# Reordering one RWKV-7 round: k's products behind the second powers, the rates' low-rank product ahead of them, the identity sums behind the state's update

## What is computed

```python
def rwkv7_scan(r, w, k, v, a, b, state):      # a = -kk, b = kk * rate, 16 heads of 64
    def step(S, inp):
        r_t, w_t, k_t, v_t, a_t, b_t = inp
        sa = jnp.einsum('bhvk,bhk->bhv', S, a_t)
        S = S * w_t[:, :, None, :] + sa[..., None] * b_t[:, :, None, :] + v_t[..., None] * k_t[:, :, None, :]
        return S, jnp.einsum('bhvk,bhk->bhv', S, r_t)
...
w_log = -jax.nn.softplus(-(rw_w0[d] + jnp.tanh(w_low[..., d, :]) @ rw_w2[d])) - 0.5
a = jax.nn.sigmoid(rw_a0[d] + a_low[..., d, :] @ rw_a2[d])      # the rate
k_d = k * (1 + (a - 1) * rw_ka)
```

## Time and profile before

| what | value |
|---|---|
| median of three executions | 2301.28 us |
| the profiled execution's own time | 2312.86 us |
| its span on the core | 2310.8 us |
| TensorE (PE) busy | 1985.9 us, 86% of the span |
| VectorE (DVE) busy | 923.6 us, 40% |
| ScalarE (ACT) busy | 687.9 us, 30% |
| GpSimd (POOL) busy | 323.1 us, 14% |
| mean granted TensorE clock | 0.917 of full |
| RWKV rounds | from 1443.4 to 1836.4 us after the span's start |

### The profile page before, as it was taken

One profiled execution on the slowest core, in us unless ns is written; L12 is line 12 of the kernel. 1 busy time (PEld: TensorE's weight loads), 2 busy tenths in 40 slices (PEclk: granted clock), 3 DMA queues, 4 the chain that ended last, 5 costly groups with the idle time before them and its releaser, 6 DMA issues. The chain is left out here.

```text
span 2310.8 us, 54088 instructions
## 1 busy us (share of the span) xinstructions
PE 1985.9 (86%) x23877; PEld 1376.1 (60%) x23877; DVE 923.6 (40%) x1660; ACT 687.9 (30%) x1509; POOL 323.1 (14%) x210
## 2 busy tenths in 40 slices
PE   6999998997979888998578798799998897977775
PEld 3777765445854444555344587788988755634443
DVE  3193235586041111111235478466767443111102
ACT  3234534574230000100133343644543312000001
POOL 1433310001401000000100245221221000000000
PEclk8999999799979998999888999799999977988888
DMA  8554533203354798678820131000000125899975
GB/s 297 188 207 146 183 145 134 86 0 110 109 217 187 255 348 323 242 267 316 303 86 27 37 104 34 3 4 4 4 4 4 58 65 217 303 385 358 359 292 182
DMA packets 133312, 380.86 MB, mean 165 GB/s; under 512 B 14394, under 2 KB 43670, under 8 KB 115926
## 3 DMA queue, kind: packets, MB, share of 16 engines
q1 hardware_dynamic: 114528, 343.82, 40.4%
q10 hardware_dynamic: 15094, 20.99, 3.0%
q0 software_dynamic: 3456, 12.58, 1.5%
HBM read 634.54 MB, written 25.95 MB: 286 GB/s over the span
## 5 line engine op out<-in xcount | busy, mean ns | idle before, releaser
L371 PE MATMUL banks<-parts 128*128 128x512 f32 (+1 forms) x1096 | 244.0, 374 | 14.6 <-POOL parts L1523 7.6
L1814 PE MATMUL banks<-arena 128*32 128x256 f32 x1696 | 218.8, 403 | 38.1 <-DMA arena<-in_exp_w_up_dram 38.1
L371 PEld LDWEIGHTS banks<-parts 128*128 128x128 f32 x1096 | 194.1, 191 | 55.0 <-POOL parts L2388 9.5
L1815 PE MATMUL banks<-arena 128*32 128x256 f32 x1696 | 218.7, 403 | 0.0
L1880 ACT ACTIVATE arena<-banks 64x256 f32<-64x256 f32 x78 | 29.7, 380 | 556.9 <-PE banks L1815 371.1
L1814 PEld LDWEIGHTS banks<-arena 128*32 128x32 f32 x1696 | 102.1, 116 | 119.1 <-DMA arena<-in_exp_w_up_dram 42.1
L371 PE MATMUL banks<-arena,ring 128*128 128x256 f32 (+2 forms) x560 | 163.9, 460 | 9.4 <-PEq L318 8.5
L379 DVE TENSOR_TENSOR arena<-banks,arena 64x256 f32<-64x256 f32 (+3 forms) x136 | 71.0, 522 | 230.5 <-ACT arena L1880 145.1
L2005 DVE COPY arena<-banks 128x256 f32<-128x256 f32 x78 | 33.1, 425 | 323.3 <-DMA y_sorted<-arena 244.0
L1836 PE MATMUL banks<-arena 128*32 128x256 f32 x1696 | 117.5, 424 | 43.2 <-DVE arena L1995 24.6
L371 PEld LDWEIGHTS banks<-arena,ring 128*128 128x128 f32 (+1 forms) x560 | 108.7, 199 | 60.9 <-issue 47.6
(11 more groups left out here) (371 smaller groups left out, 3712.6 us busy)
## 6 DMA issues: line engine op xcount, KB each, us to landing
arena<-in_exp_w_gate_dram SPq DMA_DIRECT2D x106, 1024.0 KB
arena<-in_exp_w_up_dram SPq DMA_DIRECT2D x106, 1024.0 KB
arena<-in_exp_w_down_dram SPq DMA_DIRECT2D x53, 2048.0 KB
ring<-in_exp_w_gate_dram SPq DMA_DIRECT2D x50, 1024.0 KB
ring<-in_exp_w_up_dram SPq DMA_DIRECT2D x50, 1024.0 KB
ring<-in_exp_w_down_dram SPq DMA_DIRECT2D x25, 2048.0 KB
ring<-in_w_mod_dram SPq DMA_DIRECT2D x24, 2048.0 KB, 9.0
ring<-in_ab_w_in_dram SPq DMA_DIRECT2D x10, 2048.0 KB, 13.7
```

Of the source, the lines that this page charges most:

```text
L371: m = nc.tensor.matmul(o, a, b, start=first and n == 0, stop=last and n == len(pairs) - 1)
L1814: nc.tensor.matmul(o[r:r + BLOCK, 0:256], x, up[:, k, c], start=k == 0, stop=k == KD - 1)
L1815: m = nc.tensor.matmul(o[64 + r:64 + r + BLOCK, 0:256], x, gate[:, k, c], start=k == 0, stop=k == KD - 1)
```

## The change

In `pe_round` the AK product (in segment 1 the pair AK RK) is taken and issued behind D2t, and za is taken and issued ahead of D2, in AK's old place. In `dve_round` the masks of AK (and RK) stand behind the scans of the decays; the two sums T1 are taken out of `dve_head` and put behind the state's update (and, in segment 1, behind the addition of Y). In `pool_round` a wait for the AK product is added ahead of "A ka". `act_round` is as it was.

```diff
@@ pe_round
                     both("W1 Xt", ("a", "S b"), parts=("W1", "Xt"))
-                    if seg == 1:
-                        take_pair("AK RK", "AK", "RK")
-                        both("AK RK", ("k", "a r"), parts=("AK", "RK"))
-                    else:
-                        take("AK")
-                        both("AK", ("k", "a"))
+                if front:
+                    take("za")
+                    low_rank("za", b_a2, b_al)
+                if main:
                     take("D2")
...
                         each("D2t", [("D", "Dt")], g)
-                if front:
-                    take("za")
-                    low_rank("za", b_a2, b_al)
                 if main:
+                    if seg == 1:
+                        take_pair("AK RK", "AK", "RK")
+                        both("AK RK", ("k", "a r"), parts=("AK", "RK"))
+                    else:
+                        take("AK")
+                        both("AK", ("k", "a"))
                     take_pair("D4 T2", "D4", "T2")
@@ dve_head
                         masked("RB", "RB", g, 1, "RB read")
+
+            def dve_sum():
                 for g in range(2):
                     go(vadd(now[g]["T"], now[g]["D"], stackid[:].unsqueeze(1).to_broadcast([P, 8, L])), g, "T1")
@@ dve_round
+                if front:
+                    for d in range(2):
+                        scan_decay(d)
+                if main:
                     for g in range(2):
                         masked("AK", "AK", g, 0, "AK read")
                         if seg == 1:
                             masked("RK", "RK", g, 1, "RK read")
-                if front:
-                    for d in range(2):
-                        scan_decay(d)
-                if main:
...
                 if seg == 1:
                     onto_output("Y")
+                if front:
+                    following["dve sum"]()
@@ pool_round
                 g = nc.gpsimd.tensor_tensor
+                for x in range(2):
+                    pool.wait_ge(*at_(("AK product", x)))
```

More of the change, by code:

```diff
@@ L2956, in rwkv_round @@
             return {"front": front, "pe": pe_round, "act": act_round, "dve": dve_round, "pool": pool_round, "pe decay": pe_decay,
-                    "act decay": act_decay, "pe head": pe_head, "dve head": dve_head}
+                    "act decay": act_decay, "pe head": pe_head, "dve head": dve_head, "dve sum": dve_sum}
         def rwkv_chunks():
```

## The result

The changed kernel is **slower by 1.6%**: a median of 2341.7 us in four executions (2340.4 to 2344.7) against 2303.9 for the kernel before in the same session, ratio 1.0163, 95% interval 1.0139 to 1.0186. Measured once more beside an experiment it came to 2337.7 against 2307.0, ratio 1.0137 (1.0114 to 1.0161). The forecast was 2338, range 2317 to 2357.

The account below looks back on a forecast made before the run. TensorE's in-order list was taken as the bound. Waits +9.5 and +16.5, T1 -5.4 and clock +15.3 sum to +35.9 us on the 2301.28 median: 2337, rounded to 2338, range 2317 to 2357.

Parts of the forecast that it names:

- The banks: Hand count: D4 T2 waits for za's readers in rounds 1-4; in 5-7 AK RK does, and D4 T2 for its masks.
- Rival 4: Banks turn differently from the count, D4 T2 owes no late reader, stalls ahead of D2 go: -9 us, 2292; chance 0.06.
- Segment 0: Rounds 1 to 4: D4 T2 waits for za's tanh after 3.0 us idle, +2.4 us a round, +9.5 for four.
- Segment 1: Rounds 5 to 7: AK RK idles 3.9 us, D4 T2 2.9; +5.5 us a round, +16.5 for three; round 8 zero.
- The clock: TensorE's clock falls at each of ten new idle times, 1.7 us each, less round 4's: +15.3 us, bounds 0 and +34.
- Rival 3: Bank waits, and the clock stays low twice as long after them: +53 us, 2354; chance 0.13.
- The sum: Whole kernel: waits and T1 +20.6 us plus clock +15.3 make +35.9, giving 2337, rounded to 2338.
- T1: Two sums moved behind the state's update let W1 Xt start sooner in rounds 2 to 7: -5.4 us.
- At nothing: AK's masks behind the scans, GpSimd's new wait ahead of "A ka", and round 8 were each put at no cost.
- Rival 5: Late waits exist but most time is given back later, as in stalls ahead of N or S: +5 us, 2306; chance 0.06.
- Rivals 2 and 3: Rival 2: bank waits, but the clock stays up in nearly all: +20.6 us, 2322; chance 0.17. Rival 3 has its own line.

Follow-up runs that it names:

- experiment 4: The changed kernel with only PSUM bank numbers altered, same instructions in the same order: 2305.1 us, ratio 1.0004 to the kernel before.
- experiment 3: Kernel before with the new order of AK and za in one segment only, T1 as before: rounds 1 to 4 alone 2318.0 us, rounds 5 to 8 alone 2326.3.

## Why the prediction was right

**The banks.** The count by hand held in every round: all ten waits (four, three and three) came where it put them, released by the instructions it named. Rival 4 (another turn of the banks) is out, and experiment 4 shows that the turn alone makes the loss.

**Segment 0.** D4 T2 was put at 11.6 us behind W1 Xt and 3.0 of idle time; it came at 11.85 to 12.14 and 3.12. From W1 Xt to D4 T2 the four rounds took 48.1 us against 39.0, +9.1, where +9.5 was forecast (four times 2.42 is 9.7). That the sums agree so well is in part luck: in rounds 1 and 2 the delay is 2.7 us each, and in rounds 3 and 4 only 1.8 and 2.0, because there the kernel before had lost time itself, by 1.22 us of idle time without a releaser and by the clock's fall of the earlier trace rows.

**Segment 1.** The idle times were put at 3.9 and 2.9, and came as 4.06 and 3.13; D4 T2 was put at 16.4 without the clock and came there at 17.0 in the kernel with filled waits.

**The clock.** The price of one fall was right: 1.7 us was forecast, 1.7 was measured behind D4 T2 (experiment 3), and six waits in segment 1 cost 10.5 us where six times 1.7 (10.2) was forecast. The number of falls was not right. In segment 0 four were forecast; in the changed kernel's profile the clock fell behind none of the four waits for the tanh, in its second profile behind two, in the profile of the order in segment 0 and in both profiles of the order alone behind three, in the one with filled waits behind one. The step that put the clock's fall at every wait failed there: behind the same 3.1 us it fell in twelve of 24 cases, and what decides it stays open. Rival 3 was right on one thing: in round 6 the clock stayed low through both waits, for 13.6 us. But that round's price was 4.0 us, against 3.1 and 3.3 in its neighbours, and not twice as much. The Trainium skill ("TensorE: Matmul & The Clock Gate", "A second HAM failure mode: psum-queue depth-cycling") says that a kernel cycling through PSUM banks can let TensorE idle briefly so often that its clock swings between the two levels. The trace agrees in direction: with the banks alone changed the low stretches went away. It doesn't agree at each wait.

**The sum.** +35.9 was forecast, and the rounds grew by 34.3 us in the changed kernel's profile; the medians give 37.8 and 30.7. By segment the forecast was less good than in sum: rounds 1 to 4 grew by 10.0 where 13.1 was forecast (9.5 for the waits, 5.1 for the clock, less 1.5 for T1; above all the four falls of the clock did not come), rounds 5 to 7 by 25.3 where 22.8 was forecast (16.5 + 10.2 - 3.9; D4 T2 came 17.8 us later in sum and not 16.5, and there was more idle time without a releaser), and round 8 shrank by 1.0. Two errors of some 3 us cancel, and that is luck. The forecast time itself was rounded the wrong way, 2337.2 to 2338, which changes nothing.

**T1.** Forecast -5.4. Alone it gave -6.3 (the interval reaches from -2 to -9). In the new order it gave 3.5 in the runs side by side, which is not clear of noise. TensorE's idle time ahead of W1 Xt and vt1 fell by 6.7 us in the changed profile, a little more than forecast, since round 3's went altogether, behind 1.8 us of idle time without a releaser and with the clock low.

**At nothing.** The masks behind the scans, GpSimd's wait and round 8 (8.91 us from W1 Xt to D4 T2, 9.02 before) cost nothing, as forecast. Rival 5 (time given back later) is out: N's and S's waits are what they were. Rivals 2 and 3 bound what was seen: 20.6 and 53 against the measured 31 to 38.

## What to carry to other kernels

When buffers are handed out in turn, moving a producer moves everybody's buffer: count the turn again, and for each taker name the last reader of what it takes and where that reader stands in its own engine's list. An earlier product is worth nothing while its reader's place in an in-order list stays the same, and it holds its bank all the longer. Idle times of 3 to 4 us can cost TensorE's clock on top of themselves, here 1.7 us for each fall, and 3.5 us a round beside the 6 by which D4 T2 came later; where such a wait couldn't be cured, useless matmuls in it paid.

## What was not expected

- Filling waits with 21 extra products per execution made the kernel 9 to 16 us faster than leaving them idle, and this let the clock's price be measured by itself.
- TensorE also stands still with no releaser in the profile: "issue" in the waits, at L2594 9.3 us in seven places in the changed kernel, 7.7 before, up to 1.8 each. The packet times in the traces point to what ends it. All through the rounds the DMA queue of kind "instruction" moves packets of 16 KB, 82 in the rounds of each of eleven profiles, whether these take 362 or 413 us, and 87 in the kernel with filled waits, where TensorE has more instructions. Every one of the 84 such idle times over 0.5 us in the twelve profiles ended 1.2 to 1.5 us behind the end of such a packet. So TensorE seems to wait there for its own program to arrive. No experiment tried that; what speaks for it is the fixed distance. From profile to profile such spots come and go, and the rounds' lengths with them.
- The stretch ahead of the rounds scatters as well: round 1 began between 1449.7 and 1465.6 us in the twelve profiles, though nothing ahead of it was changed.
